# A two-layer hybrid backbone on one core: last projection placed ahead of the routing logits, and mixer operands made one step early

## The reference

```python
def _rwkv7_step(S, inp):
    r_t, w_t, k_t, v_t, kk_t, a_t = inp
    sa = jnp.einsum('bshvk,bshk->bshv', S, -kk_t)
    S = S * w_t[..., None, :] + sa[..., None] * (kk_t * a_t)[..., None, :] + v_t[..., None] * k_t[..., None, :]
    y = jnp.einsum('bshvk,bshk->bshv', S, r_t)
    return S, y

def trunk_layer(h, cond, lp, rope, ctx_k, ctx_v, s0):
    ...
    m, k, v, s_final = mixing_sublayer(u, lp, rope, ctx_k, ctx_v, s0)   # ends in ... @ lp['w_out']
    h = layer_norm(ALPHA * h + g1 * m, lp['ln1_g'], lp['ln1_b'])
    u = h * (1.0 + sc2) + sh2
    f = hier_moe(u, lp)        # group logits, expert logits, top 2 of 4, gated experts
```

## Time and profile before

| what | value |
|---|---|
| median of 3 runs (lowest, highest) | 1170.13 us (1167.74, 1172.46) |
| profiled execution, its time | 1179.68 us |
| its span, 28618 instructions | 1177.9 us |
| TensorE busy | 997.7 us (85%) |
| VectorE busy | 507.0 us (43%) |
| ScalarE busy | 317.0 us (27%) |
| GpSimd busy | 95.6 us (8%) |
| mean granted clock of TensorE | 0.92 of full speed |

### The profile page before, as it was taken

The page is one execution under the profiler, slowest core; times in us unless marked ns, Lnnn a source line. Parts: engine busy times, 40 slices in busy tenths (PEclk is TensorE's granted clock), DMA queues, the critical chain, the costliest instruction groups (busy, mean ns, idle before and its releaser), DMA issues. The chain is left out here.

```text
span 1177.9 us, 28618 instructions
## 1 busy us (share of the span) xinstructions
PE 997.7 (85%) x12572; PEld 610.9 (52%) x12572; DVE 507.0 (43%) x1378; ACT 317.0 (27%) x733; POOL 95.6 (8%) x128
## 2 busy tenths in 40 slices
PE   3899999779697899999874999889878999999940
PEld 3766666667576366333324755557766465333310
DVE  0103855453625335333206338646666435333226
ACT  1231116333332022211113411265443032212110
POOL 1200000000100000123110000000010000121110
PEclk9999998898978898999996999999989899999985
DMA  9877726243626626899956314200010745899851
GB/s 357 301 215 263 246 88 245 77 168 123 236 98 169 226 86 232 294 387 374 369 196 179 134 56 127 72 2 4 3 46 5 248 167 187 286 379 382 326 212 53
DMA packets 144568, 224.44 MB, mean 191 GB/s; under 512 B 20700, under 2 KB 98761, under 8 KB 143616
## 3 DMA queue, kind: packets, MB, share of 16 engines
q1 hardware_dynamic: 131712, 185.61, 45.9%
q0 software_dynamic: 10592, 29.64, 6.9%
q10 hardware_dynamic: 2128, 7.21, 1.5%
HBM read 216.73 MB, written 21.14 MB: 202 GB/s over the span
## 5 line engine op out<-in xcount | busy, mean ns | idle before, releaser
L1545 ACT ACTIVATE region<-bank 128x512 f32<-128x512 f32 (+3 forms) x322 | 155.5, 511 | 233.7 <-PE bank L1452 73.8
L1426 PE MATMUL bank<-region 128*32 128x512 f32 x1152 | 171.3, 600 | 9.0 <-issue 6.4
L1426 PEld LDWEIGHTS bank<-region 128*32 128x32 f32 x1152 | 48.5, 111 | 112.1 <-issue 112.1
L1164 PE MATMUL bank<-u,ring 128*128 128x384 f32 x320 | 106.5, 489 | 0.0
L1330 PE MATMUL bank<-ring,u 128*128 128x512 f32 x192 | 90.7, 631 | 8.8 <-DVE u L2296 5.9
L1452 PE MATMUL bank<-ring,region 128*32 128x512 f32 x768 | 87.3, 595 | 1.4 <-ACT region L1545 1.4
L2214 DVE COPY_PREDICATED region<-lev,bank 128x256 f32<-128x256 uint8 x90 | 40.4, 449 | 101.5 <-PE bank L973 101.3
L1164 PEld LDWEIGHTS bank<-u,ring 128*128 128x128 f32 x320 | 60.0, 191 | 40.3 <-issue 1.4
L1612 ACT ACTIVATE region<-bank 128x384 f32<-128x384 f32 x50 | 23.7, 491 | 169.4 <-PE bank L1164 96.7
L1330 PEld LDWEIGHTS bank<-ring,u 128*128 128x128 f32 x192 | 38.2, 202 | 56.4 <-issue 45.7
L2429 DVE TENSOR_TENSOR region<-region,bank 128x256 f32<-128x256 f32 x24 | 10.1, 421 | 124.5 <-ACT region L1857 95.6
(11 more groups left out here) (298 smaller groups left out, 1517.0 us busy)
## 6 DMA issues: line engine op xcount, KB each, us to landing
ring<-in_w_mod SPq DMA_DIRECT2D x48, 1024.0 KB, 8.9
region<-in_moe_w SPq DMA_DIRECT2D x48, 1024.0 KB, 10.8
ring<-in_moe_w SPq DMA_DIRECT2D x48, 1024.0 KB, 12.3
ring<-in_w_in SPq DMA_DIRECT2D x20, 768.0 KB, 6.8
region<-y_rows SPq DMA_DIRECT2D x6, 1024.0 KB, 7.9
region<-g_rows POOLq DMA_DIRECT2D x4, 1024.0 KB, 6.5
ring<-in_w_in SPq DMA_DIRECT2D x12, 256.0 KB, 5.9
ring<-in_w_out SPq DMA_DIRECT2D x4, 768.0 KB, 5.4
```

The costliest lines, as they stand in the source:

```text
L1164: last = pe.matmul(dst[:, 0:T], w[:, c, tc(m)], u[:, c, :], start=(c == 0), stop=(c == KT - 1))
L1426: last = pe.matmul(bank[p % 2][cols, :], xs[:, p % 2, c, cols], of[(p * P + CTILE * q) // CAP][:, c, :], start=(c == 0), stop=(c == KT - 1))
L1545: return act.activation(dst, src, ACT.Copy)
```

## The change

It does seven things.

1. The exponentials of step s + 1 are issued on ScalarE behind levels 1, 2 and 3 of step s, two each, no longer all six behind the last.
2. Scaling is cut into three parts: behind levels 3, 4 and 5, ahead of the unmasking there.
3. The removals of step s + 1 stand between the values of step s (j by j), and go to second operand buffers. Of their results ScalarE copies the part for `at_m` (one instruction for each j), VectorE the part for the inverse (one for each j).
4. Token groups 0 and 1 are turned inside level 1, not ahead of it. The state's transposes stay where they were.
5. Values go to banks 6 and 7 and wait for the masked products of all j. Results of j = 2 go to spare columns of banks 4 and 5, and are added right behind the state; those of j = 0 and 1 follow behind the next right side, which no longer waits for all results. The right side is written over the values.
6. Unmasking is one instruction of 128x768, not two of 128x384.
7. `project_tile(2, 1)` follows `project_tile(2, 0)` at once, and tile 2 is turned ahead of the token rows of tile 0.

```diff
@@ TensorE, rwkv_step
+                def removals(of_step, j):
+
+                    pe.wait_ge(scaled_up, 2 * (l * 3 + of_step) + 1)
+                    if of_step > 0:
+                        pe.wait_ge(x_up, lev_step(l, s, LEVELS - 1, j))
...
-                tok(0)
-                tok(1)
...
+                        if k == 1 and j == 1:
+                            tok(0)
+                            tok(1)
...
-                    pe.wait_ge(msc_up, NJ * n + j + 1)
-                    pe.wait_ge(x_up, lev_step(l, s, LEVELS - 1, min(j + 1, NJ - 1)))
+                    pe.wait_ge(msc_up, NJ * (n + 1))
+                    if j == 2:
+                        pe.wait_ge(lv_cp, NJ * n + 1)
...
                 for j in range(NJ):
                     values(j)
+                    if s < 2:
+                        removals(s + 1, j)
@@ TensorE, routing
                 project_tile(2, 0)
+                project_tile(2, 1)
                 turn_tile(2 * l + 1, 1)
                 route_logits(0)
-                project_tile(2, 1)
                 route_logits(1)
+                turn_tile(2 * l + 1, 2)
                 token_rows(0)
-                turn_tile(2 * l + 1, 2)
                 token_rows(1)
@@ ScalarE, rwkv_step
+                def removals_in(of_step, j):
+
+                    act.wait_ge(a_mm, NJ * (l * 3 + of_step) + j + 1)
+                    act.activation(quads(at_m[:, j]), fresh_pairs(j, 0), ACT.Copy).then_inc(at_cp, 1)
...
-                    if s < 2 and k == LEVELS - 1:
-                        act.wait_ge(msc_mm, NJ * (n + 1))
-                        exps(s + 1, 2)
-                        exps(s + 1, 1)
-                        exps(s + 1, 0)
+                    if s < 2 and k <= 3:
+                        exps(s + 1, 3 - k)
...
-                    copy(lv_m[:, j].rearrange("p q n -> p (q n)"), bank[3 + j][:, :]).then_inc(lv_cp, 1)
+                    copy(lv_m[:, j].rearrange("p q n -> p (q n)"), value_bank(j)[:, :]).then_inc(lv_cp, 1)
+                    if s < 2:
+                        removals_in(s + 1, j)
@@ VectorE, rwkv_step
+                    if s < 2 and k >= 3:
+                        scaled(l, s + 1, k - 3)
                 if s < 2:
-                    scaled(l, s + 1)
+                    for j in range(NJ):
+                        removals_in(s + 1, j)
...
+                if s > 0:
+                    solved_for(0)
+                states(0)
+                result(0, 2)
+                solved_for(1)
+                result(0, 0)
+                result(0, 1)
+                if s < 2:
+                    states(1)
+                result(1, 2)
+                result(1, 0)
+                result(1, 1)
```

More of the change, by code:

```diff
@@ L1004, in values @@
                                     at = ((2 * hh + e) * 2 + m) * C
[L1005 removed]
+                                    last = pe.matmul(value_bank(j)[rows, at:at + C], masked_m[rows, j, 6 * e + 3 * d + which, :],
                                                      v_tok[rows, tiles(s)[d], j * P + e * C:j * P + (e + 1) * C],
@@ new lines, in solved_for, with states @@
+                    for j in range(NJ):
+                        dve.wait_ge(ry_mm, inner_step(l, sub, j))
+                        dve.wait_ge(lv_cp, NJ * n + j + 1)
+                        rest = lv_m[:, j, 4 * hh:4 * hh + 4, :].rearrange("p (e m) n -> p e (m n)", e=2)
+                        tt(rest, psum[:, 2 * j:2 * j + 2, 0:2 * C], rest, ALU.add).then_inc(rs_up, 1)
+                def states(hh):
+                    sub = 2 * s + hh
+                    for j in range(NJ):
+                        dve.wait_ge(st_mm, NJ * 5 * l + NJ * sub + j + 1)
+                        fresh = psum[:, 2 * j:2 * j + 2, 2 * C:3 * C]
+                        to = s_end if sub == 1 else s_t
+                        times = end_of(sub, j) if sub == 1 else next_of(sub, j)
+                        if sub == 0:
+                            tt(to[:, j], fresh, wide_pair(times), ALU.mult).then_inc(s_up, 1)
+                        else:
+                            link(tt(s_sum[:, j], fresh, s_t[:, j], ALU.add))
+                            tt(to[:, j], s_sum[:, j], wide_pair(times), ALU.mult).then_inc(s_up, 1)
@@ new lines, in result, with part @@
+                def result(hh, j):
+                    sub = 2 * s + hh
+                    rest = lv_m[:, j, 4 * hh:4 * hh + 4, :].rearrange("p (e m) n -> p e m n", e=2)[:, :, 1, :]
+                    if sub > 0:
+                        dve.wait_ge(rs_up, inner_step(l, sub, j))
+                    if j == 2 and sub < 5:
+                        dve.wait_ge(st_mm, NJ * 5 * l + NJ * (sub + 1))
+                    halves = range(1 if s == 0 and j < 2 else 2)
+                    def part(d):
+                        rows = rows64(parity(hh, d)) if len(halves) == 2 else slice(0, P)
+                        return (rows, y_tok[rows, tiles(s)[d], tc(j)].rearrange("p (e n) -> p e n", e=2),
+                                yo_place(j, d)[rows].rearrange("p (e n) -> p e n", e=2))
+                    if sub in (0, 2, 3):
+                        if j < 2:
+                            dve.wait_ge(yo_mm, yo_step(l, sub, j))
+                        for d in halves:
+                            rows, dst, fresh = part(d)
+                            last = tt(dst, fresh, rest[rows], ALU.add)
+                        last.then_inc(y_up, 1)
+                    elif s == 0:
+                        dve.wait_ge(y_up, step(l, 0, NJ - 1))
+                        for d in halves:
+                            rows, dst, fresh = part(d)
+                            mark(tt(dst, dst, rest[rows], ALU.add))
+                        after()
+                        if j < 2:
+                            dve.wait_ge(yo_mm, yo_step(l, sub, j))
+                        for d in halves:
+                            rows, dst, fresh = part(d)
+                            last = tt(dst, dst, fresh, ALU.add)
+                        last.then_inc(y_up, 1)
+                    else:
+                        if j < 2 or sub == 5:
+                            dve.wait_ge(yo_mm, yo_step(l, sub, j))
+                        for d in halves:
+                            rows, dst, fresh = part(d)
+                            last = tt(rest[rows], fresh, rest[rows], ALU.add)
+                        last.then_inc(y_up, 1)
+                        dve.wait_ge(y_up, y_order(l, sub, j))
+                        for d in halves:
+                            rows, dst, fresh = part(d)
+                            mark(tt(dst, dst, rest[rows], ALU.add))
```

215 lines of the change are left out of this document (105 added, 110 removed).

## The result

The changed kernel took 1174.66 us (median of 20 runs, 1164.71 to 1181.58), the kernel before 1167.53 us (20 runs, 1162.74 to 1174.12). The medians lie 7.1 us apart; the ratio on record for the two sets of runs is 1.0042, with a 95% interval of 1.0024 to 1.0060: about 5 us more, where 0.9 less was forecast. The time lies in the range of the prediction, the sign does not.

What follows compares the result with a forecast made beforehand. The mixer was taken as bound by a chain of small results passed between TensorE, VectorE and ScalarE. Mixer terms −2.3 and routing +1.4 gave −0.9 us on 1170.13, so 1169.2 us, range 1159 to 1177.

Steps and rivals of the forecast that it cites:

- rival D: Mixer step starts: TensorE only waits for VectorE, clock falls; 1.5 to 1.7 us a step, four times, about 1176; chance 0.06.
- T1: Start of step 0: first product 1.06 us earlier, token transposes bare in level 1; −0.4 a layer, −0.8 us.
- T2: Exponentials behind levels 1 to 3: free in levels 2 and 3, +0.6 us in each of four steps, +2.4.
- T3: Scaling ahead of unmasking in the levels: about +1.05 us reaches TensorE in each of layer 1's two steps, +2.1.
- T4: Scaling ahead of the last unmasking: +0.2 us twice in layer 1, +0.1 twice in layer 0, +0.6.
- T5: Values to solve, removals now between values: +1.1 us in step 0, +1.3 in step 1, two layers, +4.8.
- T6: Solve to next first product: −2.6 us (step 0 to 1), −3.5 (1 to 2), twice, −12.2; −0.7 more in layer 0.
- T7: Token transposes moved into level 1 of steps 1 and 2: +0.65 us four times, +2.6.
- T8: Step 2's new order of results gives 1.1 us; only layer 1 keeps it, −1.1.
- T9: Routing stretch, projection ahead of the logits: −0.25 us in layer 0, +1.6 in layer 1, +1.4; bounds −8.5 and +10.
- A: Routing stretch: the clock stays up, −8.5 us in place of +1.4, about 1160; chance 0.22.
- C: Routing stretch: clock at half from turning tile 1 to routing tables, both layers; +10 us for +1.4, 1178; chance 0.15.

Runs made afterwards that it cites:

- with filler: Changed kernel plus useless fp32 products of 128x256 on TensorE in the waits: 6 ahead of step 0's removals, 4 each ahead of steps 1 and 2; ratio 0.9936.
- Scaling between the updates: Changed kernel, but VectorE scales the first two parts in levels 3 and 4 between the updates of j = 1 and 2, not ahead of unmasking; ratio 1.0005.
- filler and scaling between: Changed kernel with useless products in the waits at step starts, and scaling between the updates of j = 1 and 2; ratio 0.9929, 1162.30 us.
- transposes as filler: Changed kernel with transposes in the waits at step starts, three of 128x128 for each useless product of 128x256; ratio 0.9975.
- the mixer alone: Changed kernel with the routing stretch's old order back, leaving the mixer's part of the change; ratio 1.0017.
- the tokens ahead: Changed kernel with token transposes of groups 0 and 1 back ahead of the first product, no useless products; ratio 1.0042.
- filler at steps 1 and 2 only: Changed kernel with useless products ahead of steps 1 and 2, none ahead of step 0; ratio 0.9996.
- before with filler: Kernel before the change with useless products ahead of its removals, 6 in step 0 and 4 each in steps 1 and 2; ratio 0.9982.

## Why the prediction was wrong

The forecast was a cancelling of gains and losses. The ranking of the rivals failed, and with it the sign.

**The step that failed is the clock at the starts of layer 1's steps.** The sum costed all levels 1 of that layer at full clock and put nothing in for it; only rival D named it. D had the right place and the right sign for steps 1 and 2 (the clock falls at the start of a step, because the work that filled the wait has gone), at 1.5 to 1.7 us a step, four times, and with a chance of 0.06. In the changed kernel it came about in those two steps of layer 1, at 1.8 and 2.7 us. In layer 0 it added nothing in the changed kernel's profile, since the clock was low there before. A further 2.7 us came in step 0 of layer 1, where the removals still stand and which no rival had. What hid D was its use of layer 0 as the only example: its first product ran at 0.71 there, and I added the low clock to the forecast as a gain of 0.7, from work taken out of it, without asking what the same wait would do to the clock in layer 1. The price was too small since only the first products and transposes of the three pairs were counted, where the low clock lasted through nearly all of level 1, second products and token transposes too.

**T1** held: the first product came 2.58 us behind the start of removals, with 2.84 foreseen and 3.90 before. But it rests on half a clock: the removals took 2.84 us there, and 1.63 with filler.

**T2** was somewhat high: level 2 takes 4.08 for 3.70 in steps 0 and 1 of layer 1, +0.38 and not +0.6.

**T3 and T4** were right to a tenth: level 4 takes 4.71 for 3.65 (+1.06, forecast 1.05), level 5 3.99 for 3.82 (+0.17, forecast 0.2). Scaling between the updates showed the mechanism.

**T5** was right: from values to solve 4.95 for 3.72 in step 0 (+1.2, forecast 1.1), 8.29 for 7.11 in step 1 (+1.2, forecast 1.3). The last copy of values ends a wait of 0.22, as this piece of the changed kernel has it:

```profile
810.37 0.60 ACT L1601 ACTIVATE region<-bank 128x512 f32<-128x512 f32 x1 [0.82 <-PE bank L1050]
...
811.02 0.68 PE L1095 MATMUL bank<-region 64*64 64x64 f32 x16 [0.22 <-ACT region L1601]
```

**T6** was right as a sum. Step 0 to 1 takes 11.09 for 12.62 (−1.5, forecast −2.6), partly because the state transposes run at the low clock, busy for 1.75 us (0.90 and 0.85, shown above), where they were for 1.04. Step 1 to 2 takes 10.94 for 15.08 (−4.1, forecast −3.5).

**T7** was undersized: the token transposes cost 0.97 us of level 1 and not 0.65, the time of their weight loads; their busy time is 0.88. **T8** was oversized: −0.4 (−0.24 up to the solve, −0.18 behind it) for −1.1.

Put together for layer 1: from the start of removals to the projection 113.94 us became 122.37, +8.4. The clock in the levels 1 is 7.3 of it, and the terms as measured give the other 1.2: −1.3 (T1), +2.9 (T7), +0.8, +2.1, +0.4, +2.4 (T2 to T5), −5.7 (T6) and −0.4 (T8). The same terms in the forecast came to about 0. So the sum of known costs was 1.4 us off, and the clock 7.

**T9** came out near its middle for the wrong kind of reason. Eight stretches of the old order took 39.8 to 42.5 us and 18 of the new one 39.6 to 43.9, both 40.7 on average, so 0 for +1.4. What sets them is how long the clock was at half: with 3.4 us of it they take 39.6 to 39.9 in either order, with 6.8 us 40.4 to 41.3, and with 13.7 us 42.5 to 43.9. In the changed kernel's profile it was low for a short while only:

```profile
421.76 1.96 PE L1411 MATMUL bank<-route_w,u 128*128 128x20 f32 x16 [0.53 <-ACT u L1649]
...
424.10 1.97 PE L1171 MATMUL bank<-cst,h 128*128 128x128 f32 x8
...
428.27 1.86 PE L1411 MATMUL bank<-route_w,u 128*128 128x20 f32 x16
...
430.49 0.22 DVE L2432 COPY region<-bank 128x60 f32<-128x60 f32 x1 [3.02 <-PE bank L1412]
```

Turning ran at half, the logits of tile 2 at the full clock, and the scores are read 2.9 us nearer to the projection's first half than in the earlier trace rows. In another profile, with filler and scaling between, the same stretch was at half for 10 us:

```profile
418.60:428.80 10.20, 10.09 (x47) 10.00 (x47) 2.53 (x7) 4.13 (x10) 2.66 (x1) 0.50 1.01 348
```

It took 43.8 us there. The 4.25 us that the prediction gave the order at full clock were mostly the clock of the one profile it started from. From the first product of tile 2's projection to the reading of the scores it is 26.1 us in the new order with 3.4 us at half, 27.1 in the old order with as much at half, and 26.2 in the old order at full clock. So the order is worth about 1 us there, and neither A's gain nor C's loss held. The kernel with the routing order alone measured 1.0000.

Two sums in T9 were also off by themselves: its groups add up to 441.6 and not to 441.2 (436.1 + 1.0 + 2.2 + 2.3), and its lower bound takes 4.25 twice, where layer 1 should have 1.85 less, so −6.7 and not −8.5, and rival A about 1161. Neither changes the sign.

**The rule of the Trainium skill** that transposes don't count as TensorE being busy in the same way ("TensorE: Matmul & The Clock Gate", "Part 4: PE-mode transpose") got no weight in the sum. The run with transposes as filler bears that out: its levels 1 in layer 1 stood at a clock of 1.00.

**What stays open.** Ahead of step 0 the wait is as long as before (5.57 and 5.58 us), and removals run at half in both. Yet before, the clock was back for level 1, and after, it came back only some 9 us behind the start of removals, though TensorE had no gap. It did so in the changed kernel, in the mixer alone and with scaling between. With the tokens ahead, level 1 of step 0 took 4.36. So the order of the work behind the removals may matter there. But the kernel with filler at steps 1 and 2 only has the same start of step 0 as the changed one, and took 5.49 there, and the old mixer with the new routing order took 4.41 for 3.71. So the 2.7 us of step 0 come and go with the execution, and one profile each can't tell order from chance. The same holds for the wait ahead of step 2 that left the clock at full. The mean clock of all runs is no guide either: 0.924 for the changed kernel and 0.925 to 0.927 for before. What counts is whether work or a wait stands where it is low.

## What to carry to other kernels

When work is taken out of a wait to shorten a chain, ask what TensorE does in the wait that is left. If nothing, cost the stretch behind it at half clock too, and try a few useless products there: in this kernel they turned +0.4% into −0.6%. The cost of moved instructions can be read from a trace, here to a tenth of a microsecond in T3 to T5 and to within about 1 us in the others. What they do to the clock has to be tried.

## What the runs showed that was not expected

Mean granted clock and time don't go together across kernels: before with filler has 0.939 and 0.9982, the changed one with filler 0.939 and 0.9936.

A faster mixer in layer 0 is partly given back in some kernels. The stretch from its end to tile 2's projection takes 34.4 to 35.0 us in the changed kernel and its unfilled relatives with a mixer of 156 to 161 us, and 38.8 to 40.2 in four of the seven filled ones with the new mixer. Those four wait 2.5 to 5.0 us for the output weights, as before does, and have a mean clock of 0.91 to 0.92 in the stretch; the unfilled ones wait 0 to 1.6 us and have 0.95 to 1.00. With filler and scaling between it is

```profile
369.66 6.25 PE L1397 MATMUL bank<-ring,u 128*128 128x512 f32 x10 [3.20 <-DMA ring<-in_w_out]
```

The speed of the mixer alone doesn't set it: before has 39.2 us behind a mixer of 160, and two filled kernels have 33.8 and 34.5 behind mixers of 152 and 151.
